# Feed-forward up projections of 32 weight chunks as seven block products, with weight sums made by accumulating DMAs

## What is computed

```
D_FF = 2816
def swiglu(h, w_in, w_out):          # h: 512 x 1024 (normalised, weighted x)
    gu = h @ w_in                    # w_in: 1024 x 5632
    gate, up = gu[..., :D_FF], gu[..., D_FF:]
    return (jax.nn.silu(gate) * up) @ w_out
for each of 2 layers:
    x = x + mixer(rmsnorm(x, norm_mix_w[i]))
    x = x + swiglu(rmsnorm(x, norm_ffn_w[i]), ffn_w_in[i], ffn_w_out[i])
```

## Time and profile before

| | us |
|---|---|
| runs: median of 3 (lowest to highest) | 1452.57 (1450.4 to 1454.68) |
| the profiled execution, its own time | 1452.55 |
| span of its trace | 1450.7 |
| PE busy, share of the span | 1427.9, 98% |
| DVE busy | 793.8, 55% |
| ACT busy | 593.1, 41% |
| POOL busy | 53.4, 4% |

### The profile page before, as it was taken

How to read it: one execution, slowest core, us unless ns; L and a number is a source line. 1 busy time by engine, 2 the same in 40 slices (tenths; PEclk the granted TensorE clock), 3 DMA queues, 4 the chain that set the end, 5 groups by cost and what they waited for, 6 DMA issues and landing times.

```text
span 1450.7 us, 17603 instructions
## 1 busy us (share of the span) xinstructions
PE 1427.9 (98%) x6854; PEld 1156.0 (80%) x6854; DVE 793.8 (55%) x1641; ACT 593.1 (41%) x1199; POOL 53.4 (4%) x108
## 2 busy tenths in 40 slices
PE   9999999999999999999999999999899999999998
PEld 8777767887888888888888888866688888888887
DVE  6566654675577565443454445777564443345443
ACT  6655543455454243232223334666642322223223
POOL 0111001000000000000000000001000000000000
PEclk9999999999999999999999999999999999999999
DMA  7211111223213132313332133222032222322222
GB/s 250 87 59 58 59 58 58 68 96 100 84 37 121 38 117 92 112 62 99 116 111 101 62 100 118 91 56 69 30 113 91 87 80 92 134 87 87 91 82 75
DMA packets 25922, 127.98 MB, mean 88 GB/s; under 512 B 3248, under 2 KB 5936, under 8 KB 14832
## 3 DMA queue, kind: packets, MB, share of 16 engines
q1 hardware_dynamic: 25408, 126.60, 25.9%
q10 hardware_dynamic: 432, 0.27, 0.1%
...
## 4 chain that ended last, share of the span: by engine, by line
PE 94%; DVE 3%; ACT 1%; issue 1%; DMA 0%; SPq 0%; POOLq 0%; DVEq 0%; POOL 0%; ACTq 0%
PE PS L609 92%; PE PS L882 1%; PE PS L628 1%; DVE FT L1665 1%; DVE WL L1225 1%; DVE FT L1225 0%; DMA FT<-rows 0%; DVE FT L1228 0%; PE PS L858 0%; ACT VF L964 0%; ACT L964 0%; DVE FT L1231 0%; DVE FP L1231 0%; DVE G L1225 0%; ACT FT L964 0%
## 5 line engine op out<-in xcount | busy, mean ns | idle before, releaser
L609 PE MATMUL PS<-XH,WH 128*128 128x512 f32 x1080 | 430.9, 399 | 0.9 <-ACT VF L964 0.9
L609 PE MATMUL PS<-XH,WL 128*128 128x512 f32 x1080 | 421.6, 390 | 0.0
L609 PE MATMUL PS<-XL,WH 128*128 128x512 f32 x1080 | 421.1, 390 | 0.0
L1225 DVE TENSOR_TENSOR WL<-RAW,WH 128x512 fp32r<-128x512 f32 (+1 forms) x454 | 288.6, 672 | 200.9 <-ACT WH L964 200.2
L609 PE MATMUL PS<-FR,WH 128*128 128x512 f32 (+1 forms) x1132 | 340.9, 384 | 2.0 <-DVE WL L1225 2.0
L964 ACT ACTIVATE WH<-RAW 128x512 fp32r<-128x512 f32 (+1 forms) x454 | 250.6, 608 | 177.1 <-PE PS L609 171.7
L609 PEld LDWEIGHTS PS<-FR,WH 128*128 128x128 f32 x1132 | 209.4, 189 | 44.2 <-issue 3.7
L609 PEld LDWEIGHTS PS<-XH,WH 128*128 128x128 f32 x1080 | 203.0, 188 | 47.5 <-issue 6.1
L609 PEld LDWEIGHTS PS<-XH,WL 128*128 128x128 f32 x1080 | 203.0, 188 | 43.3
L609 PEld LDWEIGHTS PS<-XL,WH 128*128 128x128 f32 x1080 | 203.3, 188 | 41.2 <-issue 1.0
L609 PE MATMUL PS<-FR,WL 128*128 128x512 f32 (+1 forms) x566 | 216.4, 382 | 0.0
(11 more groups left out here) (122 smaller groups left out, 1146.5 us busy)
## 6 DMA issues: line engine op xcount, KB each, us to landing
RAW<-in_f_in SPq DMA_DIRECT2D x44, 1024.0 KB, 4.9
RAW<-in_w_in SPq DMA_DIRECT2D x12, 1024.0 KB, 4.8
RAW<-in_m_in SPq DMA_DIRECT2D x12, 1024.0 KB, 4.9
...
RAW<-in_f_ob SPq DMA_DIRECT2D x16, 640.0 KB, 3.9
RAW<-in_a_in SPq DMA_DIRECT2D x6, 1024.0 KB, 5.0
RAW<-in_w_out SPq DMA_DIRECT2D x4, 1024.0 KB, 4.9
RAW<-in_m_out SPq DMA_DIRECT2D x4, 1024.0 KB, 4.9
```

The source lines that it names most:

```text
L609: return e.matmul(o, l, r, start=start, stop=stop, skip_group_check=True)
L1225: return e.tensor_tensor(o, a, b, op)
```

## The change

The first 6 up chunks of each layer (`PLAIN`) stay as they are. The other 16, in both layers 32, are each computed as a 2 by 2 block product by Winograd's form of Strassen's scheme: the chunk's weights are four blocks (gate or up, first or second 512 inputs), the activations four blocks (inputs by half, tokens 0 to 255 or 256 to 511), and seven products replace eight. Each product q is one PE step (`seven`): 4 k-tiles by 3 matmuls of 256 columns, 84 in all for a chunk. Products 4, 5 and 6 accumulate onto the PSUM regions of products 1, 3 and 0, after these have been read.

Around that:

- Weight sums (`ws`, on POOL): four DMAs for each chunk that add to what lies in SBUF. S1 = block 2 + block 3, added in place in `RAW` from HBM; S2 = S1 - block 0; S3 = block 2 - block 0, the addend from HBM; S4 = S2 - block 1. ACT writes the negated blocks first (`negate`, 3 for each chunk). POOL waits for S1 before it issues S2, and for S2 before S4.
- Weight splits: 7 for each such chunk, not 4. `WH` and `WL` become a ring of 8 slots of 512 columns; a slot is filled when the product 8 parts earlier is done. The ACT half ("w") and the DVE half ("v") get places of their own.
- Loads: three DMAs for the chunk's blocks (block 2; 0 and 1; 3), not one. The blocks lie in order in HBM (`pairs`, on the host).
- Activation sums, once for each layer, beside the plain chunks: DVE forms `XN` (x, norm weight and token factor multiplied, 8 tiles), four differences of 1024 columns, and their low parts; ACT their high parts (`TH`, over `G`; `TL`, over `VF`). After the last plain product, ACT and DVE overwrite `XH` and `XL` from `XN` (`bs`, 6 pieces each).
- Results: ACT copies product 1 (`s1`), DVE adds products 2, 3, 0, 5, 6 with 256-column additions (`s2`, `s3` twice, `s5`, `s6`), ACT takes two Silus of 256 columns. The factor `RB` is already in `XN`.
- The numbers in `SHIFT` are changed for other stages as well.

The diff, cut:

```diff
+PLAIN = 6
+FIRST_RING = 35
+HIGH_AT, LOW_AT = -0.25, 0.5
+NEG_AT = {2: 2, 3: 2, 6: 2}
...
 
...
-    ("qk3", 6): 2.5, ("qk3", 7): 3.5, ("qk4", 0): 3.5, ("qk4", 1): 0.5, ("qk4", 2): 1.5, ("qk4", 3): 1, ("qk4", 4): 1,
...
-        if j < 2:
...
-        return self.release[j - 2, p if same else last]
+        return self.release.get(self.before[j, p], 0)
...
+            for p in range(self.parts(j)):
+                first[j] = at = max(before + p, self.free(j, p) - 1, first.get(j, 0))
+                late, behind = (HIGH_AT, LOW_AT) if j in self.seven else (-0.25, 0)
+                self.side(at + late, ("w", j, p))
+                self.side(at + late + behind, ("v", j, p))
+        last = None
+        for j in self.seven:
+            at = self.places["w", j - 1, 0] + 3
+            self.side(at, ("ws", j))
+            for q in (2, 3, 6):
+                self.side(at if last is None else max(at, self.places["w", last, q] + NEG_AT[q]), ("ng", j, q))
+            last = j
...
+        for n, u in enumerate(order):
             self.split[u[1:]] = 11 + n
 
     def units(self):
...
         for u in sorted(self.places, key=self.places.get):
...
+                P.chunk(A["f_in"][l * 22 + half * FH + j], 8, 256, seven=half * FH + j >= PLAIN)
...
+                if x >= PLAIN:
+                    m = P.seven[j]
+                    b4 = 4 - 4 * (m % 2)
+                    for q in range(7):
+                        n = P.step(("seven", j, q, b4, P.bank.get(b4 + REGION[q], ()) if q < 4 else (), base), [j], q)
+                        if q:
+                            P.ev((f"s{q}", m, l * 22 + x, b4, n))
+                    for b, name in enumerate(("sg", "usum", "c21", "c12")):
+                        P.bank[b4 + b] = ((name, m + 1),)
...
+                    if x == PLAIN - 1:
+                        P.side(len(P.steps) - 1, *[("bs", l, i) for i in range(6)])
+                if f == FH - 1:
+                    P.ev(("fmul", l * 22 + x))
...
+            if half == 0:
+                for i in range(8):
+                    P.side(start + 8 + i // 2, ("xn", l, i))
+                for i in range(4):
+                    P.side(start + 11 + 2 * i, ("ts", l, i))
+                    P.side(start + 14 + 4 * i, ("th", l, i))
...
+    def seven_w(j, q):
+        if q in (2, 3, 6):
+            return {2: FP[:, 22, :] if P.seven[j] % 2 else STR[:, 0:512], 3: FP[:, 24, :], 6: FP[:, 23, :]}[q]
+        i = BLOCK[q]
+        return RAW[:, j % 2, 512 * i:512 * i + 512]
...
+            d, c = {1: (k, slice(0, 256)), 4: (4 + k, slice(0, 256)), 6: (4 + k, slice(256, 512))}[q]
+            return XH[:, d, c], XL[:, d, c]
+        i = {0: 0, 2: 1, 3: 2, 5: 3}[q]
+        return TH[:, i, k, :], TL[:, i, k, :]
...
                 m = mixed(t, k)
...
 
+        def seven(j, q, bank, after, base):
+            m = P.seven[j]
+            for f in after:
+                p.wait_ge(*f)
+            p.wait_ge("wl", P.split[j, q])
+            if q in (4, 5, 6):
...
+                    p.wait_ge("bsl", 6 * l + {1: k + 1, 4: 5, 6: 6}[q])
+                else:
+                    p.wait_ge("tl", 4 * l + {0: 1, 2: 2, 3: 3, 5: 4}[q])
+                o, c = region(bank, q), slice(128 * k, 128 * k + 128)
+                t = mm3(o, (WHB[:, P.slot[j, q], c], WLB[:, P.slot[j, q], c]), seven_b(q, k),
+                        q < 4 and k == 0, k == 3)
+            t.then_inc(sems["su"], 1)
+
...
+            src, high, _ = w_block(j, q)
...
+            elif q in (0, 2, 3, 6):
+                p.wait_ge({0: "s1d", 2: "s2d", 3: "s3d", 6: "s4d"}[q], 16 * (P.seven[j] + 1))
...
+            p.wait_ge("su", P.free(j, q))
+            copy(high, src).then_inc(sems["wh"], 1)
+
+        def negate(j, q):
...
+            copy(seven_w(j, q), RAW[:, j % 2, 512 * i:512 * i + 512], scale=-1.0).then_inc(sems["ng"], 1)
...
+        def s1(m, n, bank, su):
+            p.wait_ge("su", su)
+            p.wait_ge("fm", n - 1)
+            copy(FT[:, 6 + n % 2, 0:256], region(bank, 1)).then_inc(sems["p1"], 1)
...
+        def s4(m, n, bank, su):
+            p.wait_ge("su", su)
+            p.wait_ge("fm", n - 1)
+            act(FT[:, 4 + n % 2, 0:256], region(bank, 4), ACT.Silu).then_inc(sems["sg"], 1)
...
+        def s6(m, n, bank, su):
+            p.wait_ge("c12", m + 1)
+            act(FT[:, 4 + n % 2, 256:512], FT[:, 4 + n % 2, 256:512], ACT.Silu).then_inc(sems["fs"], 1)
...
+        def bs(l, i):
+            p.wait_ge("su", plain_end[l])
...
+            copy(XH[:, d, c], XN[:, d, c], scale=-1.0 if i == 5 else 1.0).then_inc(sems["bsh"], 1)
...
+        def s2(m, n, bank, su):
+            p.wait_ge("p1", m + 1)
+            p.wait_ge("su", su)
+            x = FT[:, 6 + n % 2, :]
+            tt(x[:, 256:512], x[:, 0:256], region(bank, 2), ALU.add).then_inc(sems["usum"], 1)
...
+        def s3(m, n, bank, su):
+            p.wait_ge("usum", m + 1)
...
+            tt(x[:, 0:256], x[:, 256:512], region(bank, 3), ALU.add).then_inc(sems["st"], 1)
+            p.wait_ge("st", m + 1)
+            p.wait_ge("fhl", n - 1)
+            tt(FT[:, 2 + n % 2, 256:512], x[:, 0:256], region(bank, 0), ALU.add).then_inc(sems["c22"], 1)
+
+        def s5(m, n, bank, su):
+            p.wait_ge("su", su)
+            tt(FT[:, 2 + n % 2, 0:256], FT[:, 6 + n % 2, 256:512], region(bank, 5), ALU.add).then_inc(sems["c21"], 1)
...
+        def s6(m, n, bank, su):
+            p.wait_ge("su", su)
...
+            tt(FT[:, 4 + n % 2, 256:512], FT[:, 6 + n % 2, 256:512], region(bank, 6), ALU.add).then_inc(sems["c12"], 1)
+
+        def fmul(n):
...
+            p.wait_ge("fs", n + 1)
+            if f < PLAIN:
+                p.wait_ge("fu", f + PLAIN * l + 1)
...
+            else:
+                p.wait_ge("c22", n + 1 - PLAIN - PLAIN * l)
+                p.wait_ge("c21", n + 1 - PLAIN - PLAIN * l)
+                up = x
+            tt(x, FT[:, 4 + n % 2, :], up, ALU.mult).then_inc(sems["fm"], 1)
+
+        def xn(l, d):
...
+            stt(XN[:, d, :], XT[:, d, :], SM[:, w:w + 1], RB[:, :], ALU.mult, ALU.mult).then_inc(sems["xn"], 1)
+
+        def bs(l, i):
...
+            o = stt(lo, XN[:, d, c], -1.0, h, ALU.mult, ALU.subtract) if i == 5 else tt(lo, XN[:, d, c], h, ALU.subtract)
+            o.then_inc(sems["bsl"], 1)
+
+        def tsum(l, i):
...
+
+        def th(l, i):
...
+            tt(TL[:, i, :, :], TT[i], TH[:, i, :, :].bitcast(F32), ALU.subtract).then_inc(sems["tl"], 1)
...
+        def ws(j):
+            m, c = P.seven[j], chunks[j][0]
+            s1, s2, s3, s4 = (seven_w(j, q) for q in (0, 2, 3, 6))
+            p.wait_ge(f"wb2{j % 2}", 16 * blocks(j))
+            e.dma_start(s1, c[:, 1536:2048], accum_op=ALU.add).then_inc(sems["s1d"], 16)
+            p.wait_ge("ng", 3 * m + 1)
+            p.wait_ge("s1d", 16 * (m + 1))
+            e.dma_start(s2, s1, accum_op=ALU.add).then_inc(sems["s2d"], 16)
+            p.wait_ge("ng", 3 * m + 2)
+            e.dma_start(s3, c[:, 1024:1536], accum_op=ALU.add).then_inc(sems["s3d"], 16)
+            p.wait_ge("ng", 3 * m + 3)
+            p.wait_ge("s2d", 16 * (m + 1))
+            e.dma_start(s4, s2, accum_op=ALU.add).then_inc(sems["s4d"], 16)
...
+            if j not in P.seven:
+                p.wait_ge("wl", P.read(j - 2))
...
+                e.dma_start(RAW[:, j % 2, 0:nk * wdt], ap).then_inc(sems[f"wd{j % 2}"], 16)
+                return
+            m = P.seven.get(j - 2)
+            for name, i, b in (("wb2", 2, 3), ("wd", 0, 2), ("wb3", 3, 4)):
+                if m is not None:
+                    p.wait_ge("wl", P.split[j - 2, {"wb2": 0, "wd": 4, "wb3": 5}[name]])
...
+                c = slice(512 * i, 512 * b)
+                e.dma_start(RAW[:, j % 2, c], ap[:, c]).then_inc(sems[f"{name}{j % 2}"], 16)
...
+        w = pack(fi[l], fblocks)
+        v = w.reshape(22, 128, 2, 4, 2, 128).transpose(0, 1, 4, 2, 3, 5).reshape(22, 128, 2048)
+        return np.concatenate([w[:PLAIN], v[PLAIN:]])
```

More of the change, by code:

```diff
@@ L112, in __init__, with chunk, parts, part @@
         self.chunks, self.split, self.tiles, self.freed, self.bank = [], {}, [], {}, {}
+        self.slot, self.before, self.held, self.ring, self.seven = {}, {}, {}, 0, {}
         self.steps, self.begin, self.release, self.group = [], {}, {}, {}
         self.misc, self.places = {}, {}
-    def chunk(self, ap, nk, width):
+    def chunk(self, ap, nk, width, seven=False):
+        j = len(self.chunks)
         self.chunks.append((ap, nk, width))
+        if seven:
+            self.seven[j] = len(self.seven)
+        if j < FIRST_RING:
+            self.ring = 4 * (j % 2)
+        for p in range(self.parts(j)):
+            self.slot[j, p] = self.ring % 8
+            self.before[j, p] = self.held.get(self.ring % 8)
+            self.held[self.ring % 8] = j, p
+            self.ring += 1
+    def parts(self, j):
+        nk, width = self.chunks[j][1:]
+        return 7 if j in self.seven else (nk * width + 511) // 512
+    def part(self, j, k):
```

(40 more changed lines are left out.)

171 lines of the change are left out of this document (125 added, 46 removed), and 68 rows, old and new, of the table SHIFT.

## The result

The changed kernel takes 1471.06 us (1466.49 to 1473.8), the kernel before beside it 1452.88: a ratio of 1.0123, 95% interval 1.0093 to 1.0153. It is slower by 18 us, where I forecast 22 us faster. The time is outside the range, and the way it went is rival 1.

A forecast was written before the change was run, and what follows sets the result against it. PE's stream was taken to bound the kernel: 1450.7 - 25.6 (PE) + 2 (entries) + 1.5 (tables) = 1428.6 us of span, 1430.5 us with the 1.85 around it. The range was 1424 to 1460 us.

The forecast's parts named there:

- rival 1: POOL's turn exceeds 10.08 us and sets PE's pace: 1430.5 + 28 x (turn - 10.08); chance 0.18 over 10.9, 0.11 for 10.1-10.9.
- the adding DMAs: POOL's turn per seven-product chunk: S1's and S2's landings plus one issue, 9.2 us, under PE's 10.08; bounds 4.9 and 12.9.
- break-even: The turn of POOL, 10.87 us, up to which the changed kernel would still beat the kernel before.
- 0.80 us for each of 32 chunks, 25.6 us: PE's gain in feed-forward chunks: 84 matmuls of 256 columns, 10.08 us, replace 48 of 512, 10.88 us.
- Entries: Step from plain to seven-product chunks: late copies and splits on ACT and DVE cost 1 us per layer, 2 us; bounds 0 and 4.
- Tables: Rotary-table operations on DVE in layer 0's second feed-forward half cost 1.5 us in all; bounds 0 and 4.
- Evacuation: DVE's and ACT's work in the seven-product chunks fits into 10.08 us at 70 to 80% busy, costing 0.
- The moved numbers: Changed SHIFT numbers in other stages cost 0, bounds -2 and +2, as the longest wait there totals 4.4 us.
- DMAs from POOL: Landing of POOL's 256 KB adds: 4.3 us for S1, 3.9 for S2; the skill's formula gives 2.6 us.
- Rival 3: DVE's two-input operations keep POOL from issuing, making the turn 10.6 us, 11.3 at worst: 1445 us; chance 0.03.

The follow-up runs named there:

- s1_before_s4: Changed kernel, but after waiting for S2 POOL issues the next chunk's S1 before this chunk's S4: 1449.7 us, ratio 0.9985.
- turn_much_longer: Changed kernel with four one-column powers on POOL in each turn, between the wait for S1 and the issue of S2: 1498.72 us.
- no_adds: Changed kernel without the four adding DMAs of each chunk, so four products use unsummed weights; all other work stays: 1429.4 us.
- old_shift: Changed kernel with the numbers in SHIFT as before the change, except the keys of the rotary tables: 1465.86 us.
- ahead_old_shift: Changed kernel with POOL issuing the next chunk's S1 before it waits for S2, and the old SHIFT numbers: 1433.94 us, ratio 0.9880.

## Why the prediction was wrong

**The step that failed is the adding DMAs: "The turn is 4.3 + 3.9 + 1.0 = 9.2 us, 0.9 us inside."** The form of the sum holds: two landings and the issues. Its sizes don't. In the mean of the 28 turns S1 takes 5.3 us and not 4.3, S2 4.4 and not 3.9, and the issues 0.6 + 0.8 + 0.8 = 2.2 and not 1.0: 11.9 us, where PE needs a chunk in 10. Four things stood behind that.

- The transfer. I priced an add as a load plus 0.7 us for reading the destination. It holds the DMA engines for 1.54 us where a copy takes 0.71, and S1 landed 1.5 us later than as a copy.
- The neighbours. I took each landing alone. S4 goes out 0.55 us ahead of S1, on the same queue, and that is 1.2 us of S1's 5.1 (`s1_before_s4`).
- The sum over the engines. I had "two or three times" 0.3 as an argument for the upper end only. At 0.82 busy a landing depends on what else is on the way, as `s1_before_s4` and `turn_much_longer` show from two sides.
- The issues. I put down one issue of 1.0 us for a turn. There are three steps: from each of the two landings to the next issue, 0.6 and 0.8 us, and from S4 to S1. What fills the time between a landing and the issue behind it is open. With the landings as measured and 1.0 us for issues the turn would be 10.7 us, still inside the break-even of 10.87.

**Rival 1's price was right in kind.** It gave 28 x (turn - 10.08). With the chunk rate of 11.85 that is 50 us on 1430.5, too much: these distances average 10.56 us even with plain copies, where PE hardly waits, since a layer's first ones are longer. PE's pace is the better measure. 28 x (11.67 - 10.11) = 44 us is to be compared with the 43 us between the traces of 1473.8 and 1430.64. Some 10 us of it is TensorE's clock. In the four halves before, it was never below full; after the change it went to 1.2 GHz six times in them, each time behind a stall of PE of 1.9 to 3.5 us. One of them, in windows of 4 us of the changed kernel:

```profile
728.00:732.00 4.00, 1.98 (x15) 1.86 (x14) 2.97 (x6) 2.44 (x5) 1.79 (x2) 0.91 0.93 186
732.00:736.00 4.00, 4.00 (x25) 4.00 (x25) 2.36 (x5) 2.56 (x6) 0.74 (x2) 0.67 0.83 198
736.00:740.00 4.00, 4.00 (x36) 4.00 (x35) 1.90 (x3) 2.24 (x5) 1.07 (x2) 1.00 0.96 237
```

PE is idle for 2 us of the first, and in the second starts 25 matmuls in 4 us, not 36. At granted clocks of 0.91 and 0.67 the two windows lose 4 x (0.09 + 0.33) = 1.7 us. Six of these are some 10 us (an estimate). The Trainium skill, "TensorE: Matmul & The Clock Gate", section "Part 1: The HAM clock gate (the "warmup" mystery)", has the clock at 1.2 GHz when the engine has been idle, and the rows agree. I had priced PE's waits without it.

**The chance.** Over 10.9 us I gave the turn 0.18. My bounds for it were 4.9 and 12.9, the estimate near their middle, and the break-even at 10.87: spread evenly between the bounds, (12.9 - 10.87) / 8.0 = 0.25 lies above it. So the chance was somewhat low, not far off. "Against it: the estimate of 9.2 us" was no evidence, because the estimate was made of the rows in doubt.

**PE, "0.80 us for each of 32 chunks, 25.6 us".** Right, a little low. Between the kernel before and `no_adds` the four halves fall from 527.2 us to 501.7, 25.5 us, entries included. A second half gives 9.7 us for 11 chunks, 0.88 each. That is the 0.119 us pace of the earlier trace rows, not the 0.120 of the earlier trace rows. Here two starts of the changed kernel that lie 51 matmuls apart, 6.07 / 51 = 0.119 us:

```profile
719.82 0.28 PE L708 MATMUL PS<-XH,WL 128*128 128x256 f32 x1
...
725.89 0.28 PE L708 MATMUL PS<-TH,WL 128*128 128x256 f32 x1
```

**Entries, 2 us.** Right in size: a first half, with 5 such chunks, gains 3.0 us in `no_adds` where 5 x 0.88 = 4.4 were due, 1.4 for each layer. **Tables, 1.5 us.** With no adds they cost nothing (121.5 us in both layers). With them the load of the positions was what cost. **Evacuation, 0.** Right.

**The moved numbers, "0, bounds -2 and +2".** Undersized: the attention part is 3 us longer even without adds (165.2 against 162.1 us). The old numbers bring back 1.3 to 1.5 us of it. The traces settle the rest. PE is idle for 10.0 us in that part before and for 13.0 in `no_adds`, with the granted clock low for 10.2 us in both: the 3 us are waits for DVE and not the clock. With the old numbers the idle time is 10.7 and 11.2 us (`old_shift`, `ahead_old_shift`), but the clock is low for 13.6 us, which costs 1.7 us more. Why it fell once more there is open. My reason, that the longest wait there was 4.4 us in total, bounds what a better order can gain, not what another can lose.

**DMAs from POOL.** The adds landed in 3.4 to 5.5 us, the plain copies in 2.8 to 4.6, both beside other transfers. The sum of 2.0 us + bytes / 436 GB/s, 2.6 us for 256 KB (the Trainium skill, "DMA: Bandwidth & Descriptors", section "Anatomy of one DMA — SWDGE (gpsimd) path"), is below all of these; no run here shows a DMA of POOL with nothing beside it.

**Rival 3** finds nothing for it: POOL's issue takes 0.87 us or, right behind another, 1.23, and those two values repeat while DVE is 65% busy; no issue is longer than 1.27 in the changed kernel.
